# Half-slab requests in the expert stage: each half waits for the same half two slabs ahead

## The reference, cut to what matters

```python
D_MODEL = 1024; D_FF = 2816; N_EXPERTS = 8; TOP_K = 2
def swiglu(h, wg, wu, wd):
    return (jax.nn.silu(h @ wg) * (h @ wu)) @ wd
def moe_ffn(h, w_router, wg, wu, wd):
    logits = (hf @ w_router).astype(jnp.float32)
    top_v, top_i = lax.top_k(logits, TOP_K)
    gates = jax.nn.softmax(top_v, axis=-1)
    ...   # rows sorted by expert, one swiglu(xe, wg[e], wu[e], wd[e]) for each block
    out = jax.ops.segment_sum(yb * row_gate[:, None], row_tok, num_segments=n + 1)[:n]
```

## Time and profile before

| what | value |
|---|---|
| median of 3 runs | 1557.56 us (1556.2 to 1563.87) |
| the profiled execution | 1556.37 us, span 1554.7 us |
| TensorE matmul busy | 1453.1 us, 93% of the span |
| TensorE weight loads busy | 1204.3 us, 77% |
| VectorE, ScalarE, GpSimd | 18%, 13%, 8% |
| moved by DMA | 398.67 MB, mean 256 GB/s |

### The profile page before, as it was taken

How to read it: one execution, slowest core, us unless ns; L and a number is a source line. 1 busy time by engine, 2 the same in 40 slices (tenths; PEclk the granted TensorE clock), 3 DMA queues, 4 the chain that set the end, 5 groups by cost and what they waited for, 6 DMA issues and landing times.

```text
span 1554.7 us, 45985 instructions
## 1 busy us (share of the span) xinstructions
PE 1453.1 (93%) x20574; PEld 1204.3 (77%) x20574; DVE 282.7 (18%) x705; ACT 203.5 (13%) x530; POOL 130.2 (8%) x200
## 2 busy tenths in 40 slices
PE   7999999999999999999999688998889988889987
PEld 5667666666666666776999688998889988888986
DVE  2354730000000235473300000000000000000012
ACT  1245410000000024542100000000000000000000
POOL 3221116000000002121100000000000000000010
PEclk9999999999999999999999999999999999999999
DMA  9933338993333532334699999999999999999991
GB/s 258 248 117 107 103 122 266 366 323 140 117 102 108 132 102 72 108 102 136 250 327 386 354 377 358 352 351 342 362 380 361 371 368 377 369 358 376 380 373 61
DMA packets 232905, 398.67 MB, mean 256 GB/s; under 512 B 24594, under 2 KB 80538, under 8 KB 232544
## 3 DMA queue, kind: packets, MB, share of 16 engines
q1 hardware_dynamic: 215920, 346.43, 65.0%
q0 software_dynamic: 15216, 46.34, 9.3%
q10 hardware_dynamic: 1568, 2.91, 0.6%
HBM read 360.00 MB, written 37.57 MB: 256 GB/s over the span
## 4 chain that ended last, share of the span: by engine, by line
PE 92%; issue 5%; DVE 2%; ACT 1%; DMA 0%; SPq 0%; ACTq 0%; DVEq 0%
PE bank L1335 30%; PE bank L1357 15%; PE bank L1240 13%; PE bank L791 7%; PE bank L1257 6%; PE bank L1087 2%; PE bank L774 2%; PE bank L1104 2%; PE bank L760 1%; PE bank L1059 1%; PE bank L1071 1%; PE bank L745 1%; PE bank L714 1%; PE bank L1371 1%; PE bank L1077 0%
## 5 line engine op out<-in xcount | busy, mean ns | idle before, releaser
L1335 PE MATMUL bank<-arena,ring 128*64 128x108 f32 (+7 forms) x11264 | 472.4, 245 | 51.2 <-issue 50.7
L1335 PEld LDWEIGHTS bank<-arena,ring 128*64 128x64 f32 x11264 | 462.2, 137 | 61.5 <-issue 61.1
L1357 PE MATMUL bank<-arena,ring 128*64 128x108 f32 (+7 forms) x5632 | 236.1, 245 | 21.7 <-issue 21.5
L1357 PEld LDWEIGHTS bank<-arena,ring 128*64 128x64 f32 x5632 | 230.3, 137 | 26.7 <-issue 26.4
L1240 PE MATMUL bank<-hnT,ring 128*128 128x336 f32 x704 | 199.1, 447 | 1.8 <-DVE hnT L1719 1.8
L1240 PEld LDWEIGHTS bank<-hnT,ring 128*128 128x128 f32 x704 | 134.0, 190 | 67.0 <-issue 2.3
L791 PE MATMUL bank<-hnT,ring 128*128 128x336 f32 x384 | 120.1, 459 | 0.0
L2202 DVE TENSOR_TENSOR arena<-arena,bank 128x432 f32<-128x432 f32 (+15 forms) x48 | 24.6, 513 | 464.5 <-PE bank L1335 464.4
L1257 PE MATMUL bank<-arena,ring 128*128 128x336 f32 x352 | 99.6, 446 | 0.0
L791 PEld LDWEIGHTS bank<-hnT,ring 128*128 128x128 f32 x384 | 70.9, 193 | 34.9 <-issue 7.0
L1257 PEld LDWEIGHTS bank<-arena,ring 128*128 128x128 f32 x352 | 67.0, 190 | 32.4
(11 more groups left out here) (387 smaller groups left out, 1078.6 us busy)
## 6 DMA issues: line engine op xcount, KB each, us to landing
ring<-in_moe_w_gate SPq DMA_DIRECT2D x352, 256.0 KB, 5.1
ring<-in_moe_w_up SPq DMA_DIRECT2D x352, 256.0 KB, 5.3
ring<-in_moe_w_down SPq DMA_DIRECT2D x352, 256.0 KB, 5.5
ring<-in_w_in SPq DMA_DIRECT2D x16, 1024.0 KB, 6.9
ring<-in_w_gate SPq DMA_DIRECT2D x11, 1024.0 KB, 14.7
ring<-in_w_up SPq DMA_DIRECT2D x11, 1024.0 KB, 15.9
xg_rows<-arena POOLq DMA_DIRECT2D x1, 11200.0 KB, 48.8
y_rows<-arena POOLq DMA_DIRECT2D x1, 11200.0 KB, 89.5
```

Source lines behind the costliest of these rows:

```text
L1335: ins = mm(into[part, rows * fi:rows * fi + rows], weights[:, c, col:col + 64], xg[:, k0 + c, :], start=(k0 + c == 0 and fi == 0), stop=(k ...
L1357: ins = mm(bank[5 + c // 4][part, rows * (c % 4):rows * (c % 4) + rows], weights[:, col:col + 64], hid[:, f, :], start=(f == 0 and c % 4 = ...
```

## The change

A slab is now split in two halves of two transfers each. The first half still tells of its landing on `slab_here[s]`, with half of the old count; the second tells of it on one of three semaphores that were used only at the program's start (`rest_here[j % 3]`). Before SP issues the first or the second half of slab j, it waits until the same half of slab j - 2 has landed, beside the old wait for the slot. TensorE waits for each half by itself. In gate and up slabs the loop is turned so that all four column blocks use the first half of the slab (`upto = 0`), and then all use the second. In down slabs the even f uses the first half and the odd f the second, as before, and now each has its own wait.

```diff
@@ -52,6 +52,7 @@
...
 PARTS = 4
+RESTS = 3
 GU_SLABS = FC
@@ -396,6 +397,7 @@
...
         states_stored, kv_stored, outputs_stored = [sem(f"states_stored{i}") for i in range(2)], sem("kv_stored"), sem("outputs_stored")
+        rest_here, rest_seen = (ident_here, const_here, tokens_here), (16, 16, 80)
         set_up, params_psum = sem("set_up"), sem("params_psum")
@@ -470,7 +472,15 @@
...
-            def expert_slabs(k, e, rows_at):
+            def half_landed(k, j, half):
+
+                s = (MOE0 + j) % RING
+                if half:
+                    sp.wait_ge(rest_here[j % RESTS], k * (8 * PARTS * FFN_SLABS // RESTS) + (rest_seen[j % RESTS] + 8 * PARTS * (j // RESTS + 1)))
+                else:
+                    sp.wait_ge(slab_here[s], k * (8 * PARTS * FFN_SLABS // RING) + (fixed_seen[s] + 8 * PARTS * (j // RING + 1)))
+
+            def expert_slabs(k, e, rows_at, first=False, again=False):
                 for j in range(FFN_SLABS):
@@ -491,7 +501,9 @@
...
                             part = (slice(0, 128), slice(i // 2, i // 2 + 1), slice(512 * (i % 2), 512 * (i % 2) + 512))
-                        sp.dma_start(dst[part], src[part]).then_inc(slab_here[s], 16)
+                        if (i == 2 or i == 0 and not again) and not (first and j < 2):
+                            half_landed(k, j - 2, i // 2)
+                        sp.dma_start(dst[part], src[part]).then_inc(slab_here[s] if i < PARTS // 2 else rest_here[j % RESTS], 16)
@@ -499,7 +511,7 @@
...
                     e = 0
-                expert_slabs(k, e, RANK_AT[k + 1] if k < EXPERTS - 1 else None)
+                expert_slabs(k, e, RANK_AT[k + 1] if k < EXPERTS - 1 else None, first=(k == 0))
             fullest = sp.value_load(crowded[0:1, 0:1], min_val=0, max_val=8 * NT)
@@ -518,7 +530,7 @@
...
                     with sp.Fori(0, EXPERTS) as e:
-                        expert_slabs(b * EXPERTS + e, e, b * EXPERTS + e + 1)
+                        expert_slabs(b * EXPERTS + e, e, b * EXPERTS + e + 1, again=True)
                 outputs(3)
@@ -1326,16 +1338,18 @@
...
                             s = (MOE0 + j) % RING
-                            pe.wait_ge(slab_here[s], k * (16 * PARTS * FFN_SLABS // RING) + (fixed_seen[s] + 16 * PARTS * (j // RING + 1)))
                             weights = slots[s].rearrange("p (k n) -> p k n", k=nk)
-                            for fi in range(nf):
-                                for c in range(nk):
-                                    for half in range(2):
-                                        part, col = slice(64 * half, 64 * half + 64), 128 * fi + 64 * half
-                                        ins = mm(into[part, rows * fi:rows * fi + rows], weights[:, c, col:col + 64], xg[:, k0 + c, :],
-                                                 start=(k0 + c == 0 and fi == 0), stop=(k0 + c == DK - 1), skip_group_check=True)
-                                    if fi < nf - 1 or c < nk - 1:
-                                        pay(ins)
+                            for fi, c in [(fi, c) for upto in range(2) for fi in range(nf) for c in range(nk // 2 * upto, nk // 2 * (upto + 1))]:
+                                if fi == 0 and c == 0:
+                                    pe.wait_ge(slab_here[s], k * (8 * PARTS * FFN_SLABS // RING) + (fixed_seen[s] + 8 * PARTS * (j // RING + 1)))
+                                if fi == 0 and c == nk // 2:
+                                    pe.wait_ge(rest_here[j % RESTS], k * (8 * PARTS * FFN_SLABS // RESTS) + (rest_seen[j % RESTS] + 8 * PARTS * (j // RESTS + 1)))
+                                for half in range(2):
+                                    part, col = slice(64 * half, 64 * half + 64), 128 * fi + 64 * half
+                                    ins = mm(into[part, rows * fi:rows * fi + rows], weights[:, c, col:col + 64], xg[:, k0 + c, :],
+                                             start=(k0 + c == 0 and fi == 0), stop=(k0 + c == DK - 1), skip_group_check=True)
+                                if fi < nf - 1 or c < nk - 1:
+                                    pay(ins)
                             owed[0] += 1
```

## The result

The changed kernel takes 1580.4 us in the median of 4 runs, against 1558.7 us for the kernel before: a ratio of 1.0143, with a 95% interval of 1.0108 to 1.0178. It is slower, by 22 us, where 1530 us was forecast with a range up to 1572. The profiled execution is the slowest of the four, 1585.9 us, 5.5 us above the median, which is 0.02 us on each of 252 slabs.

The account below looks back on a forecast made before the run. TensorE was taken to be bound by its matmuls plus 72.2 us of late instruction fetches; 1556.4 us less 27.6 gave 1528.8, and with the median 1.2 us above the profiled run 1530 us was forecast, range 1502 to 1572.

Parts of the forecast that it names:

- What bounds the kernel: TensorE's gaps, 72.2 us in 69 places, are waits for 256-instruction blocks fetched through the DMA engines that carry the weights.
- The added wait and the loop order at 0: TensorE's one more wait for each of 264 slabs and the turned loop cost 0, at most 9.8 us.
- The hold shortens the fetch by 0.4 us: SP's hold at eight transfers shortens each instruction fetch by 0.4 us; over 69 gaps that wins 27.6 us.
- The second expert's blocks: Sign of being right: instruction blocks in the 78-row expert take 5.5 to 5.6 us in place of 5.96.
- The feed at 2.9 us a slab: Under SP's hold two slabs take a 5.8 us turn, 2.9 us each, so the feed does not set the end.
- the break-even: The feed sets TensorE's end only from 3.09 us a slab, a turn of 6.2 us for two slabs.
- the cap would bring the landing down to 4.8 us: With eight 256 KB transfers in flight at 386 GB/s, a landing takes 4.8 us, 0.4 us under today's.
- feed too slow: Rival at SP's new wait: a 6.4 us turn, 3.2 us a slab, TensorE ends 27.7 us later, 1585 us; chance 0.17.
- The lead of 29 us as a buffer: TensorE's end is 29 us behind SP's last issue, and this lead of the ring can be spent on a slower feed.

Follow-up runs that it names:

- depth 20: Changed kernel with SP's hold loosened to 20 transfers of 256 KB in flight, TensorE still waiting for halves: 1554.5 us, 0.9988 of the kernel before.
- the hold alone: Changed kernel with SP's hold kept, but TensorE waits for both halves before a slab's first product, in the old loop order: 1586.8 us, ratio 1.0188.
- single release: Changed kernel, still eight transfers in flight, but each transfer waits for its own counterpart two slabs ahead: 1541.8 us, 0.9922 of the kernel before.
- two of 512 KB: Changed kernel with each half as one 512 KB transfer in place of two of 256 KB, hold at two slabs: 1567.7 us, ratio 1.0092.
- depth seven: Changed kernel with release for each transfer, each waiting for the one seven places ahead: 1586.4 us, 1.0186 of the kernel before.
- at 6: Changed kernel with release for each transfer and six transfers in flight: 1640.5 us, 1.0545 of the kernel before.

## Why the prediction was wrong

**What bounds the kernel: right.** The gaps are TensorE's instruction fetches under the load of the weights. The run with a quarter of the weights removes all but 0.7 of 72.2 us, and the gaps end behind instruction packets. The Trainium skill's page on the runtime (Runtime: NRT & Kernel Launch, Instruction fetch mechanics), by which crossing a block is mostly hidden, does not hold here under a full load, and holds in that run.

**The added wait and the loop order at 0: right** (0.9988 at depth 20).

**The hold shortens the fetch by 0.4 us: right where it can be seen.** The second expert's blocks were forecast at 5.5 to 5.6 us; they take 90.9 / 16.5 = 5.51, and as much with the hold alone, where only 0.2 us of waits for weights are among them. In the six experts behind it the feed covers it up. Counted alike, the landing of a half fell by 0.3 us, from 6.4 to 6.1 us in the mean, so the fall of 0.4 us that was carried over to the fetch was about right, from a level that was not. That the fetch follows the landing is not shown, and the match is partly luck: from ten transfers up the fetch does not move, and the prediction's own rows pointed at that, as it took the fetch for equally long where landings were 8.6 us and 5.2 us. The Trainium skill's page DMA: Bandwidth & Descriptors (Queues, rings and completion order) says that a DMA engine takes turns between queue rows, a packet at a time. If a fetch waited for no more than its turn, whatever the depth, the second expert would have stayed at 98 us; the rows decide against it at depths of eight and less, while from ten up the depth indeed makes no difference.

**The feed at 2.9 us a slab: wrong, and this is the step that failed.** The prediction put a turn at 0.4 us + a landing of 5.2 us + 0.2 us = 5.8 us for two slabs, and the break-even at 6.2 us. The turn is 2 x 3.22 = 6.44 us over the 252 slabs, and 6.35 from 860 to 1500 us, where its terms measure 0.55 + 5.53 + 0.27 us. So all three were taken too small, and of the 0.55 us that were missing the landing makes 0.33 and SP 0.22. A half is released when the later of its two transfers is in, with the last of its 32 updates, and a turn needs the average of such landings. The 5.2 us of the earlier trace rows is a median over transfers of which three in four were counted too early, as four share a semaphore. Counted on the kernel before in the same way, from SP's first issue of each half to the half's last counted update, the mean is 5.6 us for first halves and 7.2 us for second ones, 6.4 us over both: a turn over the break-even was in sight before, though it would have come out too long. The other half of the argument, that the cap would bring the landing down to 4.8 us, took the engines to keep their 386 GB/s under it; they moved 341 GB/s from 860 to 1500 us. The experiments bear the turn out: release for each transfer at the same depth takes 2.2% off (ratio 0.9922 after 1.0143, some 34 us), and fewer issues about 0.5% (1.0092).

The break-even itself, 3.09 us a slab, was right. With 3.04 us (single release) the kernel is faster, with 3.14 (two of 512 KB), 3.22 and 3.24 (depth seven) slower by 0.9, 1.4 and 1.9%.

The rival "feed too slow" had the case: a turn of 6.4 us, 3.2 us a slab, TensorE's end 27.7 us later and 1585 us. In the profiled execution, 1585.9 us, the end is 29.6 us later (1569.0 against 1539.4); the median of 1580.4 is 5 us below it. It had a chance of 0.17, because I trusted that landings shrink when less is in flight. They do, but not in proportion (5.7, 5.3 and 4.9 us in the mean at eight, seven and six), so a cap costs rate at once.

**The lead of 29 us as a buffer: right.** SP's last issue is 51.8 us later than before (1561.9 against 1510.1), and TensorE's end only 29.6 us, as 22 us of the lead were spent.

## What to carry to other kernels

A cap on transfers in flight has a price that is read from the slowest unit it waits for: take the mean time from the first issue of a release unit until all of it has landed, and from there to the next issue, not the median of one transfer, and compare turn / units in flight with the pace that the consumer needs. Release as finely as transfers are issued; here the same cap was 1.4% slower with pairs and 0.8% faster with single transfers. And where TensorE stands still every 256 instructions with nothing that it waits for, look at the load on the DMA engines before its code.

## What the runs showed of the hardware

- Instruction fetch under load: with the DMA engines full, the six experts with gaps take 5.7 to 6.0 us for each block of 256 TensorE instructions; with 135 GB/s of traffic the fetch is hidden behind blocks of 4.36 us. TensorE goes on 1.2 to 1.6 us after the packet's end. The three quarters of the weights cost this kernel 98 us (1459.4 against 1557.2), of which the profile shows 72 as gaps and 18 as longer busy time in the expert stage.
- The weight queue's depth and rate, with 256 KB transfers: TensorE's end moves from 1524.7 us at depth 8 to 1573.6 at 7 and 1622.4 at 6, some 49 us, or 0.19 us a slab, for each transfer fewer in flight. By the medians of the runs the steps are 45 and 54 us (1541.8, 1586.4, 1640.5).
